# The last expert of a mixture-of-experts layer as its own program on TensorE: no gather behind it, gates turned ahead of its last down product, both halves of its rows copied by ScalarE

## The reference

```python
def swiglu(x, w_up, w_down):
    g, v = jnp.split(x @ w_up, 2, axis=-1)
    return (jax.nn.silu(g) * v) @ w_down

def moe_swiglu(x2, w_router, w_up, w_down):
    """Top-2-of-8 SwiGLU experts on tokens x2 (T,D); only selected (token, expert) pairs are evaluated."""
    logits = (x2 @ w_router).astype(jnp.float32)
    top_val, top_idx = lax.top_k(logits, TOP_K)
    gate = jax.nn.softmax(top_val, axis=-1)
    ...            # rows of each expert collected, swiglu of each, times gate, summed per token
```

## Time and profile before

| what | value |
|---|---|
| median of three timed runs | 1264.89 us |
| the profiled execution, its own time | 1266.41 us |
| span of the profiled execution (first to last instruction) | 1264.6 us |
| TensorE busy in the span | 97% |
| DMA engines busy from 640 to 1242 us | all of them, nearly all the time (about 426 GB/s) |
| the last piece of weights issued, landed | 1214.8, 1246.1 us |
| the last copy of ye1 to the end of the span | 1254.89 to 1264.6 us |

### The profile page before, as it was taken

How to read it: one execution, slowest core, us unless ns; L and a number is a source line. 1 busy time by engine, 2 the same in 40 slices (tenths; PEclk the granted TensorE clock), 3 DMA queues, 4 the chain that set the end, 5 groups by cost and what they waited for, 6 DMA issues and landing times.

```text
span 1264.6 us, 48991 instructions
## 1 busy us (share of the span) xinstructions
PE 1232.7 (97%) x21590; PEld 1046.6 (83%) x21590; DVE 706.1 (56%) x1639; ACT 424.5 (34%) x877; POOL 100.9 (8%) x161
## 2 busy tenths in 40 slices
PE   7999999999999999999999999999999999999997
PEld 5755567878887775556799999999999999999986
DVE  6876426557866376643554555555555555554545
ACT  5516513001002142642234343333334333333332
POOL 1270020000000045011000000000000000000001
PEclk9999999999999999999899999999999999999999
DMA  9521025253442543513799999999999999999995
GB/s 372 228 83 68 1 100 215 101 199 114 188 173 94 215 188 133 208 51 133 288 385 427 424 426 424 427 426 424 426 426 427 425 426 424 427 427 424 427 426 218
DMA packets 36571, 360.95 MB, mean 285 GB/s; under 512 B 4164, under 2 KB 5828, under 8 KB 11549
## 3 DMA queue, kind: packets, MB, share of 16 engines
q1 hardware_dynamic: 33776, 354.86, 68.0%
q10 hardware_dynamic: 2156, 3.19, 0.7%
q0 software_dynamic: 576, 2.10, 0.5%
HBM read 356.77 MB, written 3.36 MB: 285 GB/s over the span
## 4 chain that ended last, share of the span: by engine, by line
PE 80%; DMA 8%; DVE 3%; SPq 1%; issue 1%; ACT 1%; POOL 0%; DVEq 0%; ACTq 0%
PE bank L2609 25%; PE bank L1951 18%; PE bank L2626 13%; PE bank L2554 6%; DMA ring<-moe_w_dram 5%; PE bank L2323 4%; DMA memT<-moe_w_dram 3%; PE bank L2595 2%; PE bank L2311 2%; PE bank L1959 2%; PE bank L2252 1%; PE bank L2340 1%; SPq L548 1%; PE bank L2645 1%; PE bank L2132 1%
## 5 line engine op out<-in xcount | busy, mean ns | idle before, releaser
L2609 PE MATMUL bank<-R,ring 128*64 128x80 f32 x11264 | 426.7, 233 | 6.5 <-DVE ring L1840 4.4
L2609 PEld LDWEIGHTS bank<-R,ring 128*64 128x64 f32 x11264 | 404.4, 137 | 13.9 <-DVE ring L1840 11.5
L1951 PE MATMUL bank<-ring 128*128 128x128 f32 (+2 forms) x1760 | 284.5, 321 | 1.6 <-ACT ring L668 0.9
L1951 PEld LDWEIGHTS bank<-ring 128*128 128x128 f32 x1760 | 239.9, 191 | 49.1 <-issue 36.6
L2626 PE MATMUL bank<-zz,ring 128*64 128x80 f32 x5632 | 224.7, 233 | 0.0
L1013 ACT ACTIVATE ring<-ring 128x1024 f32<-128x1024 f32 x160 | 169.1, 1057 | 134.3 <-PE bank L2626 134.3
L2626 PEld LDWEIGHTS bank<-zz,ring 128*64 128x64 f32 x5632 | 207.9, 137 | 0.0
L1891 DVE SCALAR_TENSOR_TENSOR zz<-zz,bank 128x80 f32<-128x80 f32 x176 | 41.9, 238 | 166.2 <-PE bank L2609 165.3
L1840 DVE COPY ring<-ring 128x1024 f32<-128x1024 f32 x160 | 109.9, 687 | 23.0 <-DMA ring<-moe_w_dram 22.8
L1018 ACT ACTIVATE sqx<-bank 128x80 f32<-128x80 f32 x176 | 41.8, 238 | 223.0 <-PE bank L2609 222.4
L1844 DVE COPY ring<-ring 128x1024 f32<-128x1024 f32 x160 | 109.8, 686 | 0.3 <-issue 0.2
(11 more groups left out here) (352 smaller groups left out, 1131.4 us busy)
## 6 DMA issues: line engine op xcount, KB each, us to landing
ring<-moe_w_dram SPq DMA_DIRECT2D x158, 1536.0 KB, 21.3
ring<-ffn_w_dram SPq DMA_DIRECT2D x11, 3072.0 KB, 10.2
ring<-w_in_dram SPq DMA_DIRECT2D x6, 2048.0 KB, 7.3
extra<-moe_w_dram SPq DMA_DIRECT2D x8, 1536.0 KB, 22.9
ring<-w_out_dram SPq DMA_DIRECT2D x4, 2048.0 KB, 7.6
ring<-w_small_dram SPq DMA_DIRECT2D x2, 3072.0 KB, 10.4
ring<-w_x_dram SPq DMA_DIRECT2D x2, 3072.0 KB, 10.8
ring<-w_in_dram SPq DMA_DIRECT2D x2, 2144.0 KB, 15.3
```

The costliest lines, as they stand in the source:

```text
L1951: i = pe.matmul(out_ap, a, b, start=(k == 0), stop=(k == n - 1))
L2609: e = pe.matmul(pb[out_bank][c0:c0 + 64, 0:CAP], half[:, P * k + c0:P * k + c0 + 64], xg[:, k], start=(k == 0), stop=(k == KT - 1), tile_p ...
```

## The change

1. **TensorE:** the loop runs over 7 experts. The last one is written a second time behind the loop, as `expert(0, E - 1, "L")`, with an inner loop of its own. This copy has neither of the two gathers. It turns the gates behind its inner loop, ahead of the last `down`, into bank 6.
2. **ScalarE:** copies the gates to `ogT` ahead of the copy of yT0, and copies ye0 and ye1 both.
3. **DVE:** loses both `gather_half` and the copy of ye1 of the last expert. The last two `add_returned` stand together behind the copy of yT1.
4. **Banks:** the last expert gets names of its own (yT0L, yT1L, gateTL, ye0L, ye1L) in the plan, in the same banks as before, and the gates in bank 6 instead of bank 0.

```diff
@@ plan_banks
-            banks.end_loop(E)
+            banks.end_loop(E - 1)
+            banks.begin_loop()
+            add("yT0L", 4); add("yT1L", 5); add("gateTL", 6); add("ye0L", 2); add("ye1L", 3)
+            banks.end_loop(1)
@@ ScalarE
-                    if t or s:
+                    if t or s == "O":
                         stage_down(at, t)
+                if s == "L":
+                    banks.wait(act, "gateTL", turn)
+                    act.activation(ogT, ps("gateTL")[0:CAP, 0:256], ACT.Copy).then_inc(banks.drain("gateTL"), 1)
                 nm = f"yT0{s}"
...
                 act.activation(ye[:, 0:512], ps(nm)[0:CAP], ACT.Copy).then_inc(banks.drain(nm), 1)
-                if s == "" and not last:
+                if s == "L":
+                    nm = "ye1L"
+                    banks.wait(act, nm, turn)
+                    act.activation(ye[:, 512:1024], ps(nm)[0:CAP], ACT.Copy).then_inc(banks.drain(nm), 1)
+                if s == "":
...
-            expert(E - 1, E - 1, "", last=True)
-            act.wait_ge(sem["gates_turned"], 1)
-            act.activation(ogT, pb[0][0:CAP, 0:256], ACT.Copy).then_inc(sem["gates_in"], 1)
+            expert(0, E - 1, "L")
@@ VectorE
-                if s != "O":
+                if s == "":
                     gather_half("n", 0, turn)
...
                 if s == "L":
                     add_returned(1, 0)
+                    add_returned(1, 1)
...
-                dve.tensor_copy(ye[:, 512:1024], ps(nm)[0:CAP]).then_inc(banks.drain(nm), 1)
-                if s == "L":
-                    gather_half("n", 1, turn, last=True)
-                    add_returned(1, 1)
+                if s != "L":
+                    dve.tensor_copy(ye[:, 512:1024], ps(nm)[0:CAP]).then_inc(banks.drain(nm), 1)
@@ TensorE
                 def gate_tiles():
-                    nm = "gateTO"
+                    nm = f"gateT{s}"
                     banks.open(pe, nm, turn)
+                    if s == "L":
+                        pe.wait_ge(sem["picked"], E + 1)
...
-                if s:
+                if s == "O":
                     gate_tiles()
...
                     up_value(n + 1)
+                if s == "L":
+                    gate_tiles()
                 if s == "":
                     pe.wait_ge(sem["picked"], at + 2)
                     gather("n", 0, turn)
...
-            with nc.Fori(0, E, engines=[pe.engine], hint_back_edge=True) as turn:
+            with nc.Fori(0, E - 1, engines=[pe.engine], hint_back_edge=True) as turn:
                 expert(turn, turn, "")
-            pe.wait_ge(sem["e_gated"], E * HT)
-            pe.wait_ge(sem["picked"], E + 1)
-            for i in range(NT):
-                e = pe.transpose(pb[0][0:CAP, P * i:P * i + P], og[:, i], ident)
-            e.then_inc(sem["gates_turned"], 1)
-            pe.wait_ge(sem["gates_in"], 1)
-            scatter("L", "", 0, E - 1)
+            expert(0, E - 1, "L")
```

More of the change, by code:

```diff
@@ L1013, in stage_down, with expert @@
                 act.activation(st_down, part(t, 2), ACT.Copy).then_inc(sem["down_staged"], 1)
-            def expert(turn, at, s, last=False):
+            def expert(turn, at, s):
                 for t in range(HT):
@@ L1028, in expert @@
                 banks.wait(act, nm, turn)
-                if s == "":
+                if s != "O":
                     act.wait_ge(sem["y_written"], at * 16 + 1)
                 act.activation(ye[:, 0:512], ps(nm)[0:CAP], ACT.Copy).then_inc(banks.drain(nm), 1)
-                if s == "" and not last:
+                if s == "L":
[3 more added lines that the diff above has]
+                if s == "":
                     act.wait_ge(sem["down_read"], at * HT + HT)
@@ L1825, in gates_in, with gather_half @@
                 dve.tensor_copy(ogT, ps(nm)[0:CAP, 0:256]).then_inc(banks.drain(nm), 1)
-            def gather_half(name, g, turn=None, last=False):
+            def gather_half(name, g, turn=None):
                 nm = f"{name}gather{g}"
@@ L1831, in gather_half @@
                                   spread(gain(G_FFN, 1, 4 * g, 4), [P, 4, CAP]), ALU.mult).then_inc(banks.drain(nm), 1)
-                if g and not last:
+                if g:
                     dve.wait_ge(banks.drain(nm), banks.count(nm, turn, False) + 1)
@@ L1901, in expert @@
                         add_returned(*divmod(RETURN_AT.index(t), NT))
-                if s != "O":
+                if s == "":
                     gather_half("n", 0, turn)
-                o = "O" if s == "O" else ""
-                nm = f"yT1{o}"
+                nm = f"yT1{s}"
                 banks.wait(dve, nm, turn)
@@ L1911, in expert @@
                     add_returned(1, 0)
-                nm = f"ye1{o}"
-                banks.wait(dve, nm, turn)
-                if s != "O":
+                    add_returned(1, 1)
+                nm = f"ye1{s}"
+                if s != "L":
+                    banks.wait(dve, nm, turn)
+                if s == "":
                     dve.wait_ge(sem["y_written"], at * 16 + 1)
-                dve.tensor_copy(ye[:, 512:1024], ps(nm)[0:CAP]).then_inc(banks.drain(nm), 1)
-                if s == "L":
-                    gather_half("n", 1, turn, last=True)
-                    add_returned(1, 1)
+                if s != "L":
+                    dve.tensor_copy(ye[:, 512:1024], ps(nm)[0:CAP]).then_inc(banks.drain(nm), 1)
                 if s:
@@ L1928, in _ @@
                 expert(turn, turn, "")
-            expert(E - 1, E - 1, "L")
+            expert(0, E - 1, "L")
             over = dve.value_load(flag[0:1, 0:1], min_val=0, max_val=1)
@@ L2671, in expert @@
                 if s:
-                    scatter(s, s, turn, turn)
+                    scatter(s, s, 0 if s == "L" else turn, turn)
             def scatter(s, rows_of, turn, rows_turn):
```

## The result

The changed kernel takes 1271.32 us in the median of 5 runs (1270.05 to 1273.35), against 1264.42 for the kernel before beside it (1263.47 to 1265.14): a ratio of 1.005 [1.0036, 1.0064]. It is **6.9 us slower**, where no measurable difference was forecast (1264.2, range 1262.6 to 1267.0).

A forecast was written before the change was run, and what follows sets the result against it. Weights were taken to bound the kernel until the last piece lands, then the tail. Tail −1.8 plus entry 1.1 gave −0.7 us: 1264.89 − 0.7 = 1264.2 us, range 1262.6 to 1267.0.

The forecast's parts named there:

- The slack: Last expert, before the tail: TensorE can be 6.7 us late, at 3.32 us a step, before it delays anything.
- The entry: Start of TensorE's copy: two code stalls and a slower clock, 7.8 us against the slack, 1.1 us coming through.
- The 3.4 of a branch: TensorE's one earlier jump to code not at hand stood 3.4 us; used as the size of each entry stall.
- Rival C: Slower: q8 packets delay the last landing by 4.2 us, or two stalls take 5 us each; 1267.3 us, 14%.
- VectorE's wait of 2.1 us at step 20: VectorE's last expert, at 1244 us: a 2.1 us wait without producer, read as evidence of cold code behind a loop.
- The packets on the weights: Entry: three q8 code packets, 4.2 us on one DMA engine, delay the last weights by 0.6 to 0.9 us.
- The other reading of the same part: Last expert, 1222 and 1227 us: two 8 KB code packets each delay the weights' landing by 0.7 us.
- The tail: After the last landing: gathers gone and copies moved give 1.8 us, VectorE's adds ending last.
- The 2.0 named for the scatter: Tail: the first scatter starts 2.03 us earlier, at 1253.45 instead of 1255.48.
- ScalarE's copy of ye1: Tail: moving this copy to ScalarE costs nothing until it is 1.3 us late for scatter 1.
- Rival D: End of span: last store no longer meets a q8 packet and lands 1.4 us sooner; 1261.7 with hidden entry, 9%.

The follow-up runs named there:

- e5: The changed kernel with the prefetch hint at VectorE's expert loop taken off; 1267.06 us, 1.0021 of the kernel before.
- e6: e3 with 13 products nobody reads added ahead of the last expert's inner loop, making TensorE 9.9 us late; 1269.54 us, 1.0038 of the kernel before.
- e10: e3 with 6 products nobody reads added ahead of the last expert's inner loop, making TensorE 4.7 us late; 1261.71 us, 0.9976 of the kernel before.
- e1: The changed kernel with the prefetch hint at TensorE's expert loop taken off; 1263.86 us, 0.9991 of the kernel before.
- e3: The changed kernel without TensorE's expert-loop hint and without the aligned head of the last expert's inner loop; 1263.52 us, 0.9994 of the kernel before.
- e2: The changed kernel without the aligned head of the last expert's inner loop, hint kept; 1263.01 us, 0.9985 of the kernel before.
- e4: e3 with the hint at VectorE's expert loop taken off too; 1263.37 us, 0.999 of the kernel before.
- e9: e4 with SyncE waiting for the last piece of weights before its branch on the flag; 1261.62 us, 0.9971 of the kernel before.
- e12: The kernel before with VectorE's hint off and SyncE waiting for the last piece before its branch; 1263.3 us, ratio 0.999.
- e7: e3 with VectorE's and ScalarE's expert-loop hints off too, so no hint is left; 1263.22 us, 0.9992 of the kernel before.
- e8: The kernel before with the hints at VectorE's and ScalarE's expert loops off; 1264.19 us, ratio 1.0.
- e11: e3 with the copy of ye1 back on VectorE between its two add_returned, instead of on ScalarE; 1264.72 us, one run.

## Why the prediction was wrong

**The slack was right.** It was 6.7 us, from steps of 3.32. In the changed kernel the inner loop starts 11.38 − 2.74 = 8.64 us late, and the clock costs 1.5 more behind it, 10.1 in all; e5 lets 3.6 through, e6's 9.88 3.3 and e10's 4.67 nothing.

**The entry was mis-sized.** The two stalls were put at 3.4 each from the branch in the earlier trace rows. The first measured 3.46. The second was 4.81, its branch 5.875. Stalls and clock were 7.8 in the prediction and measured 10.1, so 3.4 us came through and not 1.1: TensorE is ready for the product with the last piece at 1246.74 + 1.18 = 1247.92, and by the distance from the entry in the kernel before (1246.93 − 1171.11) would have begun it at 1244.48. The 3.4 of a branch was taken as the upper end of a stall and wasn't one. The load on the DMA engines doesn't explain the difference: the branch of the earlier trace rows began when they were nearly idle, the first stall lies under a share of 1.00, and the two took the same. The code packets tell where the time lies. Behind the start of its packet (1257.90, 1171.39, 1177.42) the branch or the stall ends after 2.4 to 2.6 us in all three. But the packet went out 1.0 us behind the start of the branch of the earlier trace rows and of the first stall, and 3.4 us behind the start of the branch at the aligned head (3.0 in e1). What held it back there is open. Rival C held this case (two stalls of 5 us, 1267.3) with 14%, and e5, which has the entry's cost and the tail's gain and little else, measured 1267.06.

The Trainium skill says on its page "Runtime: NRT & Kernel Launch", section "Instruction fetch mechanics", that the crossing to the next block is mostly hidden and that a taken branch outside the window stalls. The first half held in e3 (the packet at 1175.41 came without a stall) and not in the changed kernel, where straight code behind a loop with a prefetch hint stalled for 3.46 us; with the hint off it didn't (e1). The second half agrees with the 4.81 us at the aligned head, in so far as they are 0.52 without the alignment (e2).

**The failed step is the one that was left out.** The prediction used VectorE's wait of 2.1 us at step 20 as evidence on TensorE, and didn't ask what hid it. In the kernel before, that wait ends at 1246.04 and the last piece lands at 1246.10: the cover was 0.06 us. A VectorE without it would have waited 0.95 for the tanh (e4), so it had used up all of its lead. In the kernel before, the wait begins at 1243.91, 2.2 us ahead of the landing; in the changed kernel at 1249.99 − 4.26 = 1245.73, 2.05 behind the landing at 1243.68. So it stands bare, and it is longer too:

```profile
DVE zz L1894 <- issue: 4.3, 1, 4.3
PE bank L2616 <- DVE ring L1848: 2.8, 1, 2.8
```

The first is VectorE's longest wait from 1243 us to the end, the second TensorE's wait behind it. It cost TensorE 3.0 us (1247.92 to 1250.88), and the clock at 1.2 GHz from 1251.3 to 1254.7, behind that wait, 1.6 more: from that product to the last `down` it is 5.69 us (1250.88 to 1256.57), and in e3 4.04 (1247.00 to 1251.04). e5 takes both away and gains 4.5. This is the larger half of the loss, and no case of the prediction held it.

**The packets on the weights:** 0.6 to 0.9 us were allowed, 4.2 in rival C. The landing is 75.0 us behind the entry with three q8 packets in the entry (changed), with one (e3) and with none (before), so they cost nothing. The other reading of the same part, 0.7 us for each of the two 8 KB packets, was right and is worth 1.4 (e9, e12).

**The tail was right to 0.05 us.** 1.8 was forecast with VectorE's adds as the last thing; landing to last add fell from 13.81 to 11.98 (e3, e4, e7, e10), landing to the first scatter by 1.82. The 2.0 named for the scatter was 0.2 too much: in e3 the last `down` starts 0.15 behind its input and not 0.05, `turn_back` 1.39 behind `down` and not 1.26, the scatter 1.38 behind that and not 1.31. ScalarE's copy of ye1 is never waited for.

**Rival D** is in part what e3, e7 and e10 show in their profiles: the last store lands 3.0 to 3.1 us behind its issue instead of 4.3, and the span ends 3.4 to 3.5 behind the last add instead of 4.70. But its reason isn't shown. A q8 packet goes out within the last store in every one of these kernels, 1.8 to 2.5 us behind its issue in those three and 1.2 to 1.4 in most of the slower ones (before, changed, e1, e4, e5, e6, e9); in e8, e11 and e12 it is 2.4 to 2.7 and the store still takes 4.4 to 4.7. What decides is open, and the medians don't tell the two kinds apart.

**The sum.** Entry 3.4, VectorE's code 3.0, the clock behind it 1.6, the tail −1.8, the end of the span 0.5 (5.18 − 4.70): 6.7 us, where 6.75 was measured between the profiles and 6.9 between the medians. What stays open is why VectorE's wait took 2.13 us in the kernel before and 4.1 to 4.3 in the changed kernel and e6. The packets narrow it down. In all three the wait ends 1.7 to 1.8 us behind the start of the last code packet in it (1244.31, 1248.23, 1247.14). That packet went out 0.4 us behind the start of the wait in the kernel before, and 2.5 and 2.3 in the other two, with another 8 KB packet ahead of it (1247.52, 1245.66). So the 2 us more lie ahead of the packet, as at TensorE's aligned head, and not in it; what holds it back wasn't tried.

## What to carry to other kernels

Code that is split off behind a loop is cold on its engine: unroll or copy a last turn only with a look at each engine's branch and at the loop's prefetch hint, and take the hint off where what follows matters more than the back edge. Here the hint on TensorE's loop gave nothing back: the last expert's first product stands at 1171.24 without it (e3) and at 1171.11 with it (before), in two profiles that both have the 10.2 us of low clock at 617 us. A wait that ends just ahead of the thing that bounds the kernel is a debt and not evidence: for each engine write down its lead over the bound, then ask what it is once its producer comes late. And a queue engine that has nothing more to do should be kept from running on to its next branch while the weights still come in.

## What was unexpected of the hardware

- With the prefetch hint on the expert loop, the straight code behind it was fetched only when TensorE got there, 3.3 to 3.5 us of standstill; without it, a packet came in the loop's first turn, 465 us ahead (704.21 against 1169.52), and there was none.
- The jump to an aligned loop head cost 4.8 us, with the code packet going out 3.0 to 3.4 us behind the start of the branch; the same loop head without alignment cost 0.5 or nothing. Behind the packet's start TensorE went on after 2.4 to 2.6 us, with the DMA engines full or nearly idle.
- The same missing code cost VectorE 1.9 to 2.1 us with TensorE inside its slack (before, e1, e2) and 4.1 to 4.3 with it later than that (changed, e6).
- Two 8 KB code packets in a window in which all 16 DMA engines are full delayed the last transfer by 1.4 us; three packets of TensorE's queue in such a window, 60 to 72 us ahead of its landing, by nothing.
- TensorE's clock fell to 1.2 GHz for 10.2 us around the two stalls, for 6.8 around one of them (e1, e2), and for 3.4 behind the wait of 2.6 to 2.8 us in the tail (changed, e6).
